# The seams of the feed-forward, and 16 rows with high and low part in one stationary operand

## The chip, the core and the metric

The kernel runs on one core of a Trainium2 chip. The metric is the time of one execution in microseconds (us) on the device. Five engines work side by side and wait for each other through semaphores: PE multiplies matrices, DVE, ACT and POOL work on elements, SP issues the transfers.

## The reference

1024 tokens of width 1024 get 16 learned rows in front (the meta rows), 1040 rows in all. Everything is float32.

```python
h = concatenate([meta, x])                       # 1040 x 1024
y = conformer_mixer(h, ...)                      # (c * silu(z)) @ w_out + b_out
h = layer_norm(ALPHA * h + y)
y = gla_mixer(h, ...)                            # u = h @ w_in, split in q, k, v, r, a1; a scan over chunks
h = layer_norm(ALPHA * h + y)[16:]
h = h + rms_norm(attention_and_pool(rms_norm(h)) @ w_out)
hn = rms_norm(h)
ff = (silu(hn @ w_gate) * (hn @ w_up)) @ w_down  # 2816 channels = 22 blocks of 128
h = h + rms_norm(ff)
e = rms_norm(p @ w_ple_proj)
out = h + sigmoid(h @ w_ple_gate) * e
```

## The kernel before, in words

**High and low parts.** A float32 product is made of three products of rounded parts: each operand is split in a high part (`xh`, a cast) and a low part (`xl`, the rest), and PE adds high x high, high x low and low x high. ACT or POOL makes a high part, DVE or POOL the low one. The stationary operand of a matmul has 128 rows and up to 128 columns, the moving one up to 512 columns.

**Token tiles.** `TILES` holds one tile of 16 rows (the meta rows) and eight of 128. A tile's rows are the columns of the stationary operand. For tile 0 PE takes 128 columns as for all others; only 16 rows of the product are used.

**The convolution's output** (`conv_out_*`). PE multiplies the gated rows by `w_out`, tile by tile, each into two PSUM banks (`CO_BANK`). Tiles 0 and 1 are cut into pieces (`early`, `rest`), and the steps of the variance over channels (`variance_parts`, `_sums`, `_spread`) stand between them; DVE and ACT turn these into mean, root and SiLU for the later chunks of columns (`CHUNKS4`). DVE then adds the residual and the bias and makes the layer norm of each tile (nine steps, L1013 to L997), in the order of tiles. PE turns the finished tile (`turn`, through one pair of banks), ACT and DVE make high and low part (`high`, `low`). Every order is written out by hand; a semaphore counts the steps of each kind.

**GLA's values** (`gla_in_*`). For each of four heads PE makes nine token tiles of 256 columns (`token_tile`), ACT copies them out. Keys are turned and multiplied by the values into a state (`gla_tensor`); for the meta rows over 16 rows.

**The feed-forward** (`ffn_*`). 22 blocks of 128 channels. Block 0 is made the usual way. Blocks are then taken in pairs of half-size products over sums of operands (seven products in place of eight; `OP_AT`, `ACT_OF`, `sum_h`, `sum_l`). `body(i)` makes the seven products of one round and, between them, the 16 down products (`down(p, n)`) of the block before; DVE adds these to `ff_acc` (`add_down`), and gives PSUM free (`dn_left`). `body` runs 20 times, 18 of them in a loop. `ff_low` makes the low half of a block's activations on DVE, after ACT's high half. At the entry DVE also makes four sums (`sum_begin`, `sum_rest`); at the exit the last block's 16 down products follow without anything between them, then p is embedded (`embed`), the first row tile normed and turned, and multiplied by `w_ple_gate`, split by ACT (`ple_high`) and POOL (`ple_l`, 16 operations at L2563). Then each of the eight row tiles goes through turn, product, sigmoid and output.

## Time and profile before

| | |
|---|---|
| time, median of 3 runs | 2177.44 us (2175.85 to 2179.28) |
| time of the profiled execution | 2184.11 us |
| its span, first to last instruction | 2182.4 us |
| mean granted clock of TensorE | 0.995 |
| PE busy | 2136.0 us, 98% |
| PE weight loads | 1847.7 us, 85% |
| DVE, ACT, POOL busy | 1264.2, 810.4 and 1031.2 us |

Times in rows are us from the start of the span. A line number is that of the kernel before. A row of the order of time gives start, duration, engine, line, operation, output and inputs, and in brackets how long the engine stood before it and who ended that. Matmuls overlap: the duration of one is longer than the distance to the next. The granted clock is a share of the full 2.4 GHz; 0.5 is the lower level, 1.2 GHz.

### The profile page before, as it was taken

The page shows a single profiled execution, that of the slowest core. Times are in us where ns is not written, and L with a number is a line of the kernel's source. Part 1 is how long each engine was busy: PE and PEld are TensorE (multiplying, and loading weights), DVE is VectorE, ACT ScalarE, POOL GpSimd, SP SyncE. Part 2 cuts the span into 40 slices and gives each one's busy share as a digit, 9 for nine tenths or more (in the row PEclk, how much of TensorE's full clock was granted, in tenths as well). Part 3 has the DMA queues.
Part 4 walks back from the last instruction along what each step waited for, and adds up shares of the span by engine and source line. Part 5 has one row for each costly group of instructions (what it writes and reads, how often), then busy time and mean ns, then how long its engine had stood idle before and what let it go on. Part 6 is the DMA issues. An engine that isn't in the chain of part 4 may idle for free.

```text
span 2182.4 us, 31664 instructions
## 1 busy us (share of the span) xinstructions
PE 2136.0 (98%) x12224; PEld 1847.7 (85%) x12224; DVE 1264.2 (58%) x1668; ACT 810.4 (37%) x1319; POOL 1031.2 (47%) x718
## 2 busy tenths in 40 slices
PE   6999999999999999999999999999999999999898
PEld 6999987899999998888787778878888888888687
DVE  1899998900039975640016545866656666566753
ACT  3444554112148852220226754432222222222453
POOL 1788950142237745022295630255555655555500
PEclk9999999999999999999999999999999999999999
DMA  4111122421100024221302022111111111112321
GB/s 139 41 57 39 41 94 73 124 72 39 40 20 1 1 78 145 80 75 39 117 1 84 2 97 106 49 39 57 49 58 58 38 57 49 58 58 64 138 78 48
DMA packets 128555, 136.65 MB, mean 63 GB/s; under 512 B 7008, under 2 KB 113248, under 8 KB 128318
## 3 DMA queue, kind: packets, MB, share of 16 engines
q1 hardware_dynamic: 128446, 135.11, 18.9%
q8 instruction: 79, 1.29, 0.2%
q14 instruction: 30, 0.25, 0.0%
HBM read 118.29 MB, written 16.81 MB: 62 GB/s over the span
## 4 chain that ended last, share of the span: by engine, by line
PE 88%; POOL 3%; DVE 3%; issue 2%; ACT 2%; DMA 1%; SPq 0%; POOLq 0%; ACTq 0%; DVEq 0%
PE PS L369 47%; PE PS L2590 18%; PE PS L1932 3%; POOL side_sum L582 2%; PE PS L1972 2%; PE PS L1943 2%; PE PS L1985 2%; PE PS L408 2%; PE PS L419 2%; PE PS L2313 1%; PE PS L1234 1%; PE PS L1267 1%; PE PS L1645 1%; POOL wl L345 1%; PE PS L391 1%
## 5 line engine op out<-in xcount | busy, mean ns | idle before, releaser
L2779 DVE TENSOR_TENSOR ff_acc<-ff_acc,PS 128x512 f32<-128x512 f32 x336 | 226.5, 686 | 191.9 <-PE PS L369 191.3
L369 PE MATMUL PS<-xh,wh 128*128 128x352 f32 (+2 forms) x944 | 287.7, 336 | 5.1 <-DVE xl L481 4.0
L369 PE MATMUL PS<-xl,wh 128*128 128x352 f32 (+2 forms) x944 | 285.9, 334 | 0.0
L369 PE MATMUL PS<-xh,wl 128*128 128x352 f32 (+2 forms) x944 | 285.4, 334 | 0.0
L2515 POOL TENSOR_TENSOR xl<-raw,xh 128x512 fp32r<-128x512 f32 x120 | 164.4, 1378 | 140.4 <-ACT xh L2644 140.4
L627 DVE SCALAR_TENSOR_TENSOR PS<-glu,conv_vec,PS 128x1040 f32<-128x1040 f32 (+2 forms) x196 | 228.5, 1236 | 1.1
L369 PE MATMUL PS<-wh,xh 128*128 128x256 f32 (+1 forms) x744 | 217.0, 314 | 1.3 <-ACT r_silu L1537 0.6
L369 PE MATMUL PS<-wl,xh 128*128 128x256 f32 (+1 forms) x744 | 215.8, 313 | 0.0
L369 PE MATMUL PS<-wh,xl 128*128 128x256 f32 (+1 forms) x744 | 215.3, 312 | 0.0
L369 PEld LDWEIGHTS PS<-xh,wh 128*128 128x128 f32 x944 | 174.9, 188 | 13.2 <-issue 5.8
L369 PEld LDWEIGHTS PS<-xl,wh 128*128 128x128 f32 x944 | 174.6, 188 | 8.0
L369 PEld LDWEIGHTS PS<-xh,wl 128*128 128x128 f32 x944 | 174.4, 188 | 7.7
L350 POOL CAST wh<-raw 128x2048 fp32r<-128x2048 f32 x15 | 28.5, 1897 | 300.4 <-PE PS L369 143.8
L2644 ACT CAST xh<-raw 128x512 fp32r<-128x512 f32 x120 | 72.5, 619 | 236.9 <-PE PS L2590 142.1
L345 POOL TENSOR_TENSOR wl<-raw,wh 128x2048 fp32r<-128x2048 f32 x30 | 138.8, 4628 | 34.7 <-ACT wh L341 33.5
L369 PEld LDWEIGHTS PS<-wh,xh 128*128 128x128 f32 x744 | 138.8, 188 | 10.7 <-ACT v_meta L1145 1.1
L369 PEld LDWEIGHTS PS<-wh,xl 128*128 128x128 f32 x744 | 140.1, 188 | 9.2
L369 PEld LDWEIGHTS PS<-wl,xh 128*128 128x128 f32 x744 | 139.8, 188 | 9.3
L2507 POOL TENSOR_TENSOR raw<-raw 128x512 f32<-128x512 f32 x80 | 115.2, 1441 | 48.7 <-DMA raw<-in_w_ffn_up_dram 42.7
L369 PE MATMUL PS<-dnh,ffh 128*128 128x512 f32 x336 | 131.7, 392 | 3.1 <-POOL dnl L2520 2.8
L369 PE MATMUL PS<-dnh,ffl 128*128 128x512 f32 x336 | 131.3, 391 | 0.0
L369 PE MATMUL PS<-dnl,ffh 128*128 128x512 f32 x336 | 131.3, 391 | 0.0
(426 smaller groups left out, 4952.2 us busy)
## 6 DMA issues: line engine op xcount, KB each, us to landing
rows<-h_rows SPq DMA_DIRECT2D x24, 512.0 KB, 3.4
dn_raw<-in_w_ffn_down_dram SPq DMA_DIRECT2D x22, 512.0 KB, 3.5
raw<-in_gla_w_in_dram SPq DMA_DIRECT2D x10, 1024.0 KB
raw<-in_w_ffn_gate_dram SPq DMA_DIRECT2D x20, 512.0 KB
raw<-in_w_ffn_up_dram SPq DMA_DIRECT2D x20, 512.0 KB
raw<-in_conv_w_in_dram SPq DMA_DIRECT2D x16, 512.0 KB
raw<-in_w_in_dram SPq DMA_DIRECT2D x8, 1024.0 KB
h_rows<-rows SPq DMA_DIRECT2D x16, 512.0 KB, 2.6
```

The costliest lines, as they stand in the source:

```text
L345: nc.gpsimd.tensor_tensor(wl[slot][:], raw_of(u)[0][:], wh[slot][:].bitcast(F32), ALU.subtract).then_inc(unit_ready, 1)
L369: last = nc.tensor.matmul(out_of(c, cn), s, x[:, c0:c0 + cn], start=n == 0 and m == 0, stop=n == len(terms) - 1 and m == 2)
L408: ins = nc.tensor.matmul(PS[:, bank + half, :], act_of(k), w_of(k)[:, half * HALF:(half + 1) * HALF], start=first and k == 0, stop=last an ...
L419: last = nc.tensor.transpose(blocks(bank)[:, k, 0:rows], src[0:rows, k * P:(k + 1) * P], ident[0:rows, 0:rows])
L582: ins = nc.gpsimd.tensor_tensor(acc[:], acc[:], tap_part[n % 3][:], ALU.add)
L627: ins = nc.vector.scalar_tensor_tensor(out=y, in0=x, scalar=w, in1=y, op0=ALU.mult, op1=ALU.add)
L1932: return nc.tensor.matmul(out, x, w[:, k, cols], start=begin, stop=end)
L2507: nc.gpsimd.tensor_tensor(out, a, b, op).then_inc(pool_own.sem, 1)
L2515: nc.gpsimd.tensor_tensor(lo, OP_AT[o], hi.bitcast(F32), ALU.subtract).then_inc(unit_ready, 1)
L2590: ins = nc.tensor.matmul(PS[:, OP_BANK[o], :], s[:, k, :], x[:, k, :], start=k == 0 and m == 0, stop=k == 3 and m == 2)
L2644: nc.scalar.copy(ring(o)[0], OP_AT[o]).then_inc(unit_hi, 1)
L2779: nc.vector.tensor_tensor(x, x, PS[:, dn_bank(p, n), :], ALU.add).then_inc(dn_left, 1)
```

## The change

It has three parts.

**The meta rows.** The 16 rows' high part, 16 columns of zeros and their low part stand side by side in one stationary operand of 48 columns (`conv_meta`, `h1_meta`). Multiplied by the high and by the low part of the weights it gives two row groups of the product, which are added later: for the convolution's output ACT copies the second group out (`meta_shift`), POOL adds the bias, DVE adds both; for the values they stay apart (`v_meta` has 48 rows), and the keys are stored twice, with zeros between, so that the product over 48 rows adds them. Tile 1's pieces now stand where tile 0's did, banks 0 and 6 change places, and the first turns go through bank 0.

**The entry of the feed-forward.** DVE makes the first low half of block 1's activations before the last step of the fourth sum.

**The exit.** The last block's down products are issued in pieces, with `embed(0)` after ten and `turn(0)` after fourteen of them. DVE and ACT take their steps in that order (`last_down`, `last_low`). `ple_high(act, 1)` comes after the first norm; `p_h`, the activations of the last stage and its banks lie elsewhere.

```diff
@@ -13,6 +13,7 @@
 D = 1024
 SEQ = 1024
 META = 16
+MROWS = 48
...
@@ -125,8 +126,11 @@
         raw_d = at("raw_d", [P, KT, T], A0)[:, :, CHUNKS4[3][0]:CHUNKS4[3][0] + UNIT]
         CO_SLOTS = (0, 5, 1, 2)
         MID_TURN = {4: 4, 6: 6, 7: 4}
-        CO_BANK = (0, 6, 4, 2, 0, 4, 2, 0, 4)
+        CO_BANK = (6, 0, 4, 2, 6, 4, 2, 6, 4)
+        turn_bank3 = lambda t: 0 if t < 6 else 6
         slot3 = [silu_z[:, :, c:c + P] for c in (0, 128, 272, 400, 528, 656)]
+        meta_shift = silu_z[0:META, :, 784:784 + P]
+        conv_meta = at("conv_meta", [P, KT, T + PAD], Z0, F32R)[:, :, 48:48 + MROWS]
...
@@ -142,12 +146,13 @@
...
-        v_meta = at("v_meta", [META, D], S0 + 2 * SLOT + 6144)
+        v_meta = at("v_meta", [MROWS, D], S0 + 2 * SLOT + 6144)
...
+        h1_meta = at("h1_meta", [P, KT, MROWS], W0 + 8192 + 2048, F32R)
...
@@ -209,11 +214,11 @@
...
-        p_h = at("p_h", [P, 2, SEQ], Z0 + 32768, F32R)
+        p_h = at("p_h", [P, 2, SEQ], O0 + 20480, F32R)
...
@@ -817,6 +822,10 @@
...
+            act.wait_ge(gated_lo, 1)
+            nc.scalar.copy(conv_meta[:, :, 0:META], xh[:, :, 0:META])
+            nc.scalar.copy(conv_meta[:, :, META:32], glu[:, :, 0:32 - META])
+            nc.scalar.copy(conv_meta[:, :, 32:MROWS], xl[:, :, 0:META]).then_inc(meta_packed, 1)
...
+            act.wait_ge(dense_done, 1)
+            act.wait_ge(conv_gated, len(CHUNKS4))
+            nc.scalar.copy(meta_shift, blocks(CO_BANK[0])[32:MROWS]).then_inc(meta_packed, 1)
...
+            pool.wait_ge(gain_in, 48)
+            pool.wait_ge(meta_packed, 2)
+            nc.gpsimd.tensor_tensor(meta_shift, meta_shift, gain3[0][0:META], ALU.add).then_inc(meta_packed, 1)
...
@@ -875,7 +890,7 @@
             def turn(t):
                 pe.wait_ge(h1_done, t + 1)
                 after(pe, part_lo, t, H1)
-                turn_blocks(rows3[t % 3], TILES[t][1], 6).then_inc(turned, 1)
+                turn_blocks(rows3[t % 3], TILES[t][1], turn_bank3(t)).then_inc(turned, 1)
...
+            def meta(ks):
+
+                for k in ks:
+                    for w in range(2):
+                        for half in range(2):
+                            ins = nc.tensor.matmul(PS[0:MROWS, bank_of(0) + half, :], conv_meta[:, k, :],
+                                                   of_slots(CO_SLOTS, k)[w][:, half * HALF:(half + 1) * HALF],
+                                                   start=k == 0 and w == 0, stop=k == KT - 1 and w == 1)
+                if ks[-1] == KT - 1:
+                    ins.then_inc(dense_done, 1)
...
-            early(0, xh, 0, first=True)
-            early(0, xh, 1)
+            early(1, xh, 0, first=True)
+            early(1, xh, 1)
             mean_last(pe, 1, 4, 2)
             mean_last(pe, 3, 3)
-            early(1, xh, 0, first=True)
-            early(1, xh, 1)
+            pe.wait_ge(gated_lo, 1)
+            early(1, xl, 0)
             variance_parts(pe, 1)
-            pe.wait_ge(gated_lo, 1)
-            early(0, xl, 0)
+            pe.wait_ge(meta_packed, 1)
+            meta(range(3))
             variance_sums(pe, 1)
-            early(1, xl, 0)
+            meta(range(3, 4))
             variance_parts(pe, 2)
             variance_spread(pe, 1)
             pe.wait_ge(unit_ready, U_CO + 4)
-            rest(0, range(4, 6))
+            meta(range(4, 6))
             variance_sums(pe, 2)
             variance_parts(pe, 3)
             variance_spread(pe, 2)
             variance_sums(pe, 3)
-            rest(0, range(6, KT))
+            meta(range(6, KT))
             rest(1, range(4, 6))
             variance_spread(pe, 3)
             rest(1, range(6, KT))
@@ -942,6 +968,7 @@
...
+                    pe.wait_ge(meta_packed, 2)
...
+                if t == 8:
+                    pe.wait_ge(dense_left, 8)
...
+                if t == 0:
+                    dve.wait_ge(meta_packed, 3)
+                dve_own.step(dve, nc.vector.tensor_tensor(x[0:n], x[0:n], gain3[0] if t else meta_shift, ALU.add))
                 layer_norm_rows(dve, x, n, t + 1, gain3[1], gain3[2]).then_inc(h1_done, 1)
...
-                    token_tile(h % 2, c0, 3 + q % 3).then_inc(gv_tile, 1)
+                    if t == 0:
+                        pe.wait_ge(meta_packed, 4)
+                    (token_tile(h % 2, c0, 3 + q % 3) if t else meta_tile(h % 2, 3 + q % 3)).then_inc(gv_tile, 1)
+
+        def meta_tile(slot, bank):
+
+            for k in range(KT):
+                for w in (wh, wl):
+                    last = nc.tensor.matmul(PS[0:MROWS, bank, 0:UNIT], h1_meta[:, k, :], w[slot][:, k, :],
+                                            start=k == 0 and w is wh, stop=k == KT - 1 and w is wl)
+            return last
 
...
+            dve.wait_ge(dense_done, 9)
+            nc.vector.tensor_copy(h1_meta[:, :, 0:META], xh[:, :, 0:META])
+            nc.vector.tensor_copy(h1_meta[:, :, 32:MROWS], xl[:, :, 0:META])
+            nc.vector.memset(h1_meta[:, :, META:32].bitcast(F32), 0.0).then_inc(meta_packed, 1)
...
-                    nc.scalar.copy(dst, PS[0:n, 3 + q % 3, 0:GV]).then_inc(gv_left, 1)
+                    nc.scalar.copy(dst, PS[0:n if t else MROWS, 3 + q % 3, 0:GV]).then_inc(gv_left, 1)
...
-                        last = nc.tensor.matmul(out_bank(6, h), k_rows[c % 2][0:n, h, :], v[:, h * GV:(h + 1) * GV], start=True, stop=True)
+                        last = nc.tensor.matmul(out_bank(6, h), k_rows[c % 2][0:n if c else MROWS, h, :], v[:, h * GV:(h + 1) * GV], start=True, stop=True)
...
-            nc.scalar.copy(k_rows[c % 2][0:n].rearrange("p h t -> p (h t)"), PS[0:n, 0, :]).then_inc(k_rows_done, 1)
+            for r in (32, 0) if c == 0 else (0,):
+                last = nc.scalar.copy(k_rows[c % 2][r:r + n].rearrange("p h t -> p (h t)"), PS[0:n, 0, :])
+            last.then_inc(k_rows_done, 1)
...
+            nc.gpsimd.memset(k_rows[0][0:MROWS], 0.0)
...
-            for n in range(HALVES):
-                down(LAST, n)
...
+                if last:
+                    act.wait_ge(p_turned, 1)
+                    nc.scalar.copy(p_h[:].rearrange("p k t -> p (k t)"), banks(0, 4)).then_inc(p_ready, 1)
...
-            ple_high(act, 1)
...
+                if n == 4:
+                    ff_low(1, 0, A_)
...
+            def last_low(i):
+                last_down(dve, 0, 2)
+                ff_low(i + 2, 1, C_)
+                last_down(dve, 2, 6)
...
-                ff_low(i + 2, 1, C_)
+                if last:
+                    last_low(i)
+                else:
+                    ff_low(i + 2, 1, C_)
...
-            ff_low(1, 0, A_)
...
-            body(FPAIRS - 3)
-            add_down(LAST, 0, 12)
+            body(FPAIRS - 3, True)
...
-            add_down(LAST, 12, HALVES)
+            last_down(dve, 6, 10)
...
-            pe.wait_ge(gain_in, G9 + 32)
+                turn_row(ff_acc[:, j, :], P, 2).then_inc(h4_turned, 1)
+
+            def act_cols(x, k):
+                return x[:, k // 4, (k % 4) * P:(k % 4 + 1) * P]
+
+            for n in range(10):
+                down_last(pe, n)
             pe.wait_ge(p_ready, 2)
             pe.wait_ge(w_low, DN0 + 2 * FPAIRS + 1)
+            embed(0)
+            for n in range(10, 14):
+                down_last(pe, n)
+            turn(0)
+            for n in range(14, HALVES):
+                down_last(pe, n)
+            pe.wait_ge(matrix_lo, M9 + 4)
+            pe.wait_ge(dn_left, 2 + LAST * HALVES + 14)
+            pe.wait_ge(act9_hi, 1)
+            dense_stage(lambda k: act_cols(act9h[0], k), lambda k: ple_h[k // 4][:, k % 4, :], out_bank9(0), first=True)
+            pe.wait_ge(act9_lo, 1)
+            dense_stage(lambda k: act_cols(act9l[0], k), lambda k: ple_h[k // 4][:, k % 4, :], out_bank9(0))
+            turn(1)
+            dense_stage(lambda k: act_cols(act9h[0], k), lambda k: ple_l[k // 4][:, k % 4, :], out_bank9(0), last=True).then_inc(dense_done, 1)
+            embed(1)
             pe.wait_ge(dn_left, 2 + FPAIRS * HALVES)
-            embed(0)
-            turn(0)
-            pe.wait_ge(matrix_lo, M9 + 4)
-
-            pe.wait_ge(act9_hi, 1)
-            dense_stage(lambda k: act9h[0][:, k, :], lambda k: ple_h[k // 4][:, k % 4, :], 0, first=True)
-            dense_stage(lambda k: act9h[0][:, k, :], lambda k: ple_l[k // 4][:, k % 4, :], 0)
-            turn(1)
-            pe.wait_ge(act9_lo, 1)
-            dense_stage(lambda k: act9l[0][:, k, :], lambda k: ple_h[k // 4][:, k % 4, :], 0, last=True).then_inc(dense_done, 1)
-            embed(1)
             for j in range(1, NX):
                 if j + 1 < NX:
                     turn(j + 1)
...
+            ple_high(act, 1)
...
+            last_down(dve, 10, HALVES)
+            low(0)
...
```

## Rows read from the trace of the kernel before

**Rows 1.** The page's first part: busy time and share of the span of each engine

```profile
...
PE 2136.0 (98%) x12224; PEld 1847.7 (85%) x12224; DVE 1264.2 (58%) x1668; ACT 810.4 (37%) x1319; POOL 1031.2 (47%) x718
...
```

**Rows 2.** Busy time (and count) of each engine from 1800 to 2000 us, with clock and DMA

```profile
...
1800.00:2000.00 200.00, 200.00 (x873) 162.26 (x872) 121.89 (x178) 51.24 (x91) 115.43 (x87) 1.00 0.18 53
...
```

**Rows 3.** The chain of work, 290 to 445 us: start, us, what

```profile
...
344.74 11.12 PE PS L369 x48
...
428.44 7.68 PE PS L369 x48
...
```

**Rows 4.** The chain of work, 440 to 660 us

```profile
...
521.45 7.57 PE PS L391 x48
...
538.87 68.42 PE PS L369 x576
...
```

**Rows 5.** PE in order of time, 1422 to 1445 us; in brackets the idle time and its end

```profile
...
1424.51 0.39 PE L2590 MATMUL PS<-xh,xl 128*128 128x512 f32 x1
1427.65 0.77 PE L369 MATMUL PS<-dnh,ffh 128*128 128x512 f32 x1 [2.75 <-POOL dnl L2520]
...
1434.04 0.40 PE L2590 MATMUL PS<-sum_h,xh 128*128 128x512 f32 x1
...
```

**Rows 6.** PE in order of time at the end of the feed-forward

```profile
...
2037.21 0.70 PE L369 MATMUL PS<-xl,ffh 128*128 128x512 f32 x2 [1.32 <-DVE ffl L2788]
...
2052.29 0.77 PE L369 MATMUL PS<-xl,p_h 128*128 128x512 f32 x1 [2.74 <-DVE ff_acc L2779]
...
2061.46 5.50 PE L408 MATMUL PS<-ple_h,act9h 128*128 128x512 f32 x16 [2.42 <-ACT act9h L2950]
...
```

**Rows 7.** The engines in a stretch of 2 us; the granted clock stands before the DMA share

```profile
...
1430.00:1432.00 2.00, 2.00 (x6) 1.57 (x5) 0.07 (x1) 0.00 (x0) 1.84 (x3) 0.50 0.00 0
...
```

**Rows 8.** ACT in order of time, 290 to 470 us

```profile
...
323.00 2.78 ACT L780 ACTIVATE conv_sq<-glu 128x3072 f32<-128x3072 f32 x1 [0.40 <-DVE glu L740]
...
335.66 0.17 ACT L789 ACTIVATE stat<-PS 128x3 f32<-128x3 f32 x1 [2.76 <-PE PS L718]
...
357.03 2.77 ACT L771 CAST xh<-glu 128x3072 fp32r<-128x3072 f32 x1 [4.74 <-DVE glu L755]
...
428.48 1.01 ACT L1029 CAST xh<-PS 128x1024 fp32r<-128x1024 f32 x1 [3.21 <-PE PS L426]
...
```

**Rows 9.** POOL in order of time, 290 to 360 us

```profile
...
291.72 2.02 POOL L589 TENSOR_TENSOR tile_sum<-tile_sum,glu 128x1040 f32<-128x1040 f32 x1
...
```

**Rows 10.** DVE in order of time, 355 to 470 us

```profile
...
360.19 1.20 DVE L1013 SCALAR_TENSOR_TENSOR silu_z<-silu_z,PS 16x1024 f32<-16x1024 f32 x1
...
429.53 1.23 DVE L1006 TENSOR_TENSOR xl<-PS,xh 128x1024 fp32r<-128x1024 f32 x1 [1.66 <-ACT xh L1029]
430.67 1.21 DVE L1013 SCALAR_TENSOR_TENSOR silu_z<-silu_z,PS 128x1024 f32<-128x1024 f32 x1
...
```

**Rows 11.** DVE in order of time, 1396 to 1452 us

```profile
...
1422.61 3.27 DVE L2760 TENSOR_TENSOR sum_l<-sum_f,sum_l 128x2048 fp32r<-128x2048 f32 x1
1425.80 2.35 DVE L2788 TENSOR_TENSOR ffl<-scratch,ffh 128x512 fp32r<-128x512 f32 x2
...
```

**Rows 12.** ACT in order of time, 1396 to 1452 us

```profile
...
1422.27 1.14 ACT L2660 CAST ffh<-scratch 128x512 fp32r<-128x512 f32 x2 [0.89 <-PE PS L369]
...
```

**Rows 13.** POOL in order of time, 1396 to 1452 us

```profile
...
1420.39 3.34 POOL L2520 TENSOR_TENSOR dnl<-dn_raw,dnh 128x512 fp32r<-128x512 f32 x1
1425.47 1.54 POOL L2520 TENSOR_TENSOR dnl<-dn_raw,dnh 128x512 fp32r<-128x512 f32 x1 [1.74 <-ACT dnh L2648]
...
```

**Rows 14.** ACT in order of time, 2014 to 2066 us

```profile
...
2039.20 3.71 ACT L2738 CAST ple_h<-ple_raw 128x2048 fp32r<-128x2048 f32 x2
...
```

**Rows 15.** DVE in order of time, 2014 to 2066 us

```profile
...
2047.48 2.28 DVE L2846 TENSOR_TENSOR xl<-PS,p_h 128x2048 fp32r<-128x2048 f32 x1
...
2053.84 2.18 DVE L2984 TENSOR_TENSOR ff_acc<-ff_acc,rows 128x1024 f32<-128x1024 f32 x1
...
```

**Rows 16.** POOL in order of time, 2014 to 2066 us

```profile
...
2033.88 23.27 POOL L2563 TENSOR_TENSOR ple_l<-ple_raw,ple_h 128x512 fp32r<-128x512 f32 x16
```

54 lines of the change are left out of this document (33 added, 21 removed).

## The prediction

> **What bounds the kernel now.** I read the page's first part, then the chain of work that ended last, then the timelines of the engines around the four places that the diff touches. PE is busy for 98% of the span [rows 1], and in the loop over the feed-forward pairs for all of it [rows 2]. So the kernel ends when PE has done its list: time can be won by matmuls that are taken out where nothing else is late, and where PE stands still. The chain through the convolution's output consists of PE alone [rows 3], and so does that through GLA's values [rows 4]. Two places have real holes: the start of the feed-forward, one wait of 2.75 us [rows 5], and its end, waits of 1.32, 2.74 and 2.42 us [rows 6]. After the long holes the granted clock is 0.5 for some us (the 1.2 GHz level of the two) [rows 7]: from 1427.65 to 1434.04 [rows 5] PE starts 15 matmuls of 512 columns, 0.426 us each, where the loop has 200 us / 872 = 0.23 us. A hole costs more than its length.
>
> **Part A, the meta tile of the convolution's output.** Before: 8 blocks x 3 products x 2 halves = 48 matmuls for 16 rows. After: the stationary operand has 48 columns (16 high, 16 zero, 16 low), so 8 x 2 x 2 = 32. The moving side keeps 512 columns, 11.12 us / 48 = 0.232 us each [rows 3]: 16 x 0.232 = 3.7 us less on PE. Three things can hold that back.
> (1) The variance steps are woven between these matmuls. Ahead of the third variance sum 12 matmuls go (60 before, 48 after), 2.8 us; but PE, 8 matmuls earlier there (about 325.3), now comes to the second big chunk's squares 0.5 us before ACT has them, 323.00 + 2.78 = 325.8 [rows 8]; so 2.3 us are left. From that sum the chain goes through the root at 335.66 [rows 8], SiLU, gate, high and low part to token tile 2. PE's own list is 3.7 - 0.5 = 3.2 us ahead there; it will wait a little for the low part: 3.1 us (2.3 if that chain is later than I think).
> (2) New steps stand in DVE's chain. The low product sits in PSUM partitions 32 to 47: ACT copies it (16x1024; the 128x1024 copy out of PSUM takes 1.01 us [rows 8]), POOL adds the bias (the nearest row is 128x1040 with 2.02 us [rows 9]), DVE waits for it. ACT's gated_high(3) would end at 357.03 + 2.77 - 2.3 = 357.5, so the sum is there at 357.5 + 1.0 + 2.0 + 0.1 = 360.6. DVE's first step began at 360.19 and took 1.20 [rows 10]; 2.3 us earlier it ends at 359.1. DVE waits 1.5 us, and its chain over the nine tiles is only 0.8 us ahead of before. It has no other hole until 427.87 (the 1.66 us in front of 429.53, [rows 10]). Bounds of the unseen POOL add: nothing, and twice 2.0 us: a chain 2.3 us ahead, or 1.2 us behind.
> (3) Does PE meet that chain? Before, part(1,0) started at 428.44 + 7.68/2 = 432.28 [rows 3], DVE freed its bank at 430.67 + 1.21 = 431.9 [rows 10]: a slack of 0.4 us, most of it because DVE itself waited 1.66 us. After: PE wants the bank at 432.28 - 3.1 = 429.2; DVE has low(6) at 427.87 - 0.8 + 1.2 = 428.2, and the bank free at 429.4. PE waits 0.2 to 0.3 us. Part A: 2.8 us; bounds 0.8 (the dear POOL add: the bank is free at 431.4, 2.2 us after PE wants it) and 3.7. The three small ACT copies that pack the operand lie in a wait of ACT for DVE, 5.2 us long before; uncovered they would cost their own 0.8 us at most (the 0.17 to 0.3 us of such small ACT rows, [rows 8]). The turns through other banks are the same transposes.
>
> **Part B, GLA's values for the meta rows.** Four heads, 24 matmuls of 256 columns become 16: 32 fewer. 68.42 us / 576 = 0.119 us each [rows 4], so 3.8 us. Whether 48 stationary columns make a matmul dearer: the 32-column narrow tile takes 7.57 / 48 = 0.158 us for 352 columns [rows 4], a little under the width's share; I take no difference. The three DVE operations that pack h1, POOL's memset and ACT's second copy of the keys lie beside a tile of 24 matmuls (2.9 us) or more. If one were uncovered I put it at 0.6 us, a half of an ACT cast twice as wide [rows 8]. Part B: 3.8, bounds 3.2 and 3.8.
>
> **Part C, the start of the feed-forward.** PE stops in front of down(1, 0), which needs the low half of the activations. DVE makes it (two 128x512 in 2.35 us from 1425.80) only after the last subtraction of sum 4 (3.27 us from 1422.61) [rows 11]. The change puts the first half in front of that subtraction. ACT has the high half at 1422.27 + 0.6 [rows 12]. The half will be there at about 1424.4, PE needs it at 1424.51 + 0.23 = 1424.74 [rows 5]: the hole goes, 1427.65 - 1424.74 = 2.9 us. With it goes the low clock, which lasted to 1434.04 [rows 5, 7]: 15 matmuls in 6.4 us instead of 3.4, 3.0 us. What is late next: the subtraction, 2.3 to 3.3 us, runs to 1426.7 or 1427.7, the second half (0.7 to 1.2) to 1427.4 or 1428.9, the first add_down (0.7) to 1429.2 if I lean to the later; down(1, 2) wants it after 18 more matmuls, at 1428.8: a wait of 0.4 us, too short for the clock (the 1.32 us hole at 2037.21 did not lower it, [rows 6]). Part C: 5.9 - 0.4 = 5.5 us. Bounds: 4.0 if PE waits again at the third and fourth operand, which POOL makes; 5.9.
> POOL and DVE slow each other here: the subtraction takes 3.27 us instead of 2.3, with POOL's dnl at the same time [rows 11, 13]. The Trainium skill, page SBUF — State Buffer, section "SBUF: two separate sides", has the two share a port pair as an exclusive lock, held for the whole instruction by whoever starts first, when DVE has two SBUF inputs. The trace agrees: POOL's dnl, queued at 1420.39, takes 3.34 us and the next 1.54 [rows 13]. By that rule the wait of 0.4 us comes; if the two didn't hinder each other, ffl(1, 1) would be there by 1427.4, down(1, 2) would not wait, and part C would be 5.9 us, the sum 16.8.
>
> **Part D, the end of the feed-forward.** The 16 down products of the last pair, embed(0) and turn(0) are now woven: ten downs, embed(0), four, turn(0), two, then the dense product. The norm of row tile 0 starts as soon as its two halves are in. I replayed it with the durations of before. PE starts at 2037.21 as before [rows 6]. ACT copies p_h before the second ffh, inside a wait for DVE; ple_high(1), 3.71 us from 2039.20 before [rows 14], now comes after the first norm, at about 2042.8. DVE: two adds, ffl, four adds, p_l (2.28, [rows 15]) to about 2045.8; PE has then waited 1.2 us for embed(0). Four adds, the norm of tile 0 (up to 2.18 us for its last step beside POOL [rows 15]) to 2052.2; PE waits 0.9 us for turn(0), then has the last two downs at 2054.5. In front of the dense product the program waits for all of ple_l. POOL makes that in 16 operations, 23.27 us from 2033.88, so to 2057.15 [rows 16]. POOL's list isn't touched and it was not waiting; the later ple_high(1) is done at 2046.5, before POOL comes to it. So PE starts the dense product at 2057.2 instead of 2061.46 [rows 6]: 4.3 us. It stands 2.7 us before that, so I take the low clock once more, as behind the 2.42 us hole of before, where 16 matmuls took 5.50 us [rows 6] instead of 16 x 0.23 = 3.7 (1.8 us, of which I count 1.7). Part D: 4.3 us. If the clock stays up, 4.3 + 1.7 = 6.0; if it stays down for 6 us as at 1428, 3.0; if DVE or POOL is 1 us later as well, 2.0. From there on all is as before, with PE full.
>
> **Sum.** 2.8 + 3.8 + 5.5 + 4.3 = 16.4 us. The profiled execution took 2184.11 us (span 2182.4 and 1.7 around it), so 2167.7; it stands 6.7 us above the median of the runs, 2177.44. I take the saving off the median: 2161.0 us. Ends: least 0.8 + 3.2 + 4.0 + 2.0 = 10.0, 2167.4; most 3.7 + 3.8 + 5.9 + 6.0 = 19.4, 2158.0.
>
> **The rivals.**
> - The clock stays high at the end (the three shorter holes don't lower it): for it, the hole of 1.32 us did not; against it, the last is 2.7 us. 18.1 us, 2159.3. Chance 0.25.
> - DVE's chain sets the convolution's output, because POOL's add or the wait in front of it is dearer, and POOL's operands come late in the first pair: A 0.8, C 4.0, D 4.3: 12.9 us, 2164.5. For it, the slacks of 0.4 us; against it, that POOL has to be late in two places at once. Chance 0.15.
> - The merged operand doesn't save what it says (a matmul with 48 stationary columns, or one that waits for its load, costs half as much again): A and B give nothing; 9.8 us, 2167.6. Against it the narrow tile [rows 4]. Chance 0.05.
> - Slower: the pair loop runs in another phase of POOL against DVE and PE gets a wait in each of its 18 turns. To undo 16.4 us and lose 4.4 us more takes 20.8 / 18 = 1.16 us a turn; from there it decides, at 1.3 us a turn the time is 2184. For it, the loop's lateness at entry changes and POOL's operations stretch beside DVE. Against it, PE has no hole in 200 us [rows 2] with POOL busy 58%, and a loop bound by PE falls back into its own phase. Chance 0.03.
> - The forecast, 2159.5 to 2163: 0.50.
>
> **The numbers.** 0.2% is 4.4 us, about what a measurement of this kernel can tell. The forecast and the first three rivals are all faster by more than that: 0.50 + 0.25 + 0.15 + 0.05 = 0.95; no difference 0.02, for what I haven't seen, slower 0.03. The range takes both ends of the sum, 2158.0 and 2167.4, and up to 1 us for the scatter of the runs (1.8 us around their median): 2157 to 2168.
>
> **What would show it.** In the profile of after: 48 matmuls fewer; token tile 2 starts about 3 us earlier, at 341.7, DVE waits about 1.5 us before its first bias add, part(1, 0) has at most a short wait; the values stage is 208 matmuls and 24.7 us a head instead of 216 and 25.7; no wait above 0.7 us between 1400 and 1430 (of the old time) and clock 1.0 there; at the end holes of about 1.2, 0.9 and 2.7 us, the last one ended by POOL's ple_l. It would be wrong with a new hole in the first pair or in the loop, or if the clock's low stretches move to other places.

## The result, and the profile after

| | runs | median, us | lowest to highest |
|---|---|---|---|
| before, on the same chip | 9 | 2180.44 | 2175.85 to 2189.18 |
| after | 9 | 2169.49 | 2167.41 to 2172.80 |

The ratio is 0.9944, 95% interval 0.9929 to 0.996: 0.56% faster, 11 us by the medians. The forecast was 16.4 us and 2161.0 us. The range ended at 2168, so the time lies 1.5 us outside it. The profiled execution of after took 2170.98 us (span 2169.3), that of before 2184.11 (2182.4): 13.1 us between them.

The first part of the page after, which answers to [rows 1]:

```profile
...
PE 2125.5 (98%) x12176; PEld 1835.9 (85%) x12176; DVE 1265.1 (58%) x1671; ACT 812.1 (37%) x1324; POOL 1034.3 (48%) x720
...
```

48 matmuls are gone, as they should be. PE was busy 10.5 us less and stood still 2.6 us less.

**Before the first edit.** The same step stands at 306.98 us before and 308.83 us after, though nothing ahead of it was changed. The 1.85 us are made at the start, where the clock fell in this execution and not in that of before. The lines give the stretch, then the busy time of PE, its loads, DVE, ACT and POOL; the granted clock is the last number but two:

```profile
...
34.00:38.00 4.00, 2.63 (x19) 2.37 (x17) 0.29 (x1) 1.33 (x2) 0.00 (x0) 1.00 0.00 0
38.00:42.00 4.00, 2.92 (x10) 2.95 (x11) 0.93 (x1) 1.93 (x2) 2.45 (x1) 0.60 0.00 0
...
```

**Part A.** The chain of work of after, 306 to 450 us, answers to [rows 3]:

```profile
...
343.59 11.38 PE PS L374 x48
...
399.10 1.03 PE PS L431 x8
...
414.92 1.06 PE PS L431 x8
...
427.98 7.96 PE PS L374 x48
...
441.52 8.63 PE PS L374 x55
```

Token tile 2 starts 1.15 us earlier by the trace, 3.0 with the 1.85 of the start. Then 0.9 us is given back in four short waits: 11.38 instead of 11.12, turns of 1.03 and 1.06 instead of 0.87, 7.96 instead of 7.68. From ACT's first gate step (308.73) to its first copy of a GLA projection (449.19) it is 140.46 us; before it was 142.50 (306.88 to 449.38). Part A gave 2.05 us. DVE and POOL in order of time show why:

```profile
...
359.77 1.20 DVE L1042 SCALAR_TENSOR_TENSOR silu_z<-silu_z,PS 16x1024 f32<-16x1024 f32 x1
363.06 1.21 DVE L1047 TENSOR_TENSOR silu_z<-silu_z 16x1024 f32<-16x1024 f32 x1 [2.09 <-POOL silu_z L855]
...
387.96 5.42 DVE L1047 TENSOR_TENSOR silu_z<-silu_z 128x1024 f32<-128x1024 f32 x1
...
```

```profile
...
360.56 2.40 POOL L855 TENSOR_TENSOR silu_z<-silu_z 16x1024 f32<-16x1024 f32 x1 [7.19 <-ACT silu_z L844]
...
387.71 4.59 POOL L350 TENSOR_TENSOR wl<-raw_z,wh 128x2048 fp32r<-128x2048 f32 x1
...
```

DVE waits 2.09 us for POOL's addition of 2.40 us on 16 rows (I had 1.5 and 2.0). With the 1.85 us of the start counted, its chain is only 0.2 us ahead of before from there on (363.06 against 361.43), where I had 0.8. 25 us later an addition that otherwise takes 1.23 us takes 5.42 beside POOL's subtraction. That one is in the kernel before too (5.43 us); it costs nothing there, and can cost something now that PE is ahead.

**Part B.** The meta tiles of GLA's values answer to [rows 4]:

```profile
...
537.69 17.32 PE PS L374 x144
555.01 1.87 PE PS L1161 x16
...
579.61 1.84 PE PS L1161 x16
...
```

16 matmuls in 1.85 us where 24 took 24 x 0.119 = 2.85. From ACT's first GLA copy to DVE's weight cast behind the values it is 182.07 us (449.19 to 631.26) instead of 186.01 (449.38 to 635.39): 3.9 us.

**Part C.** DVE at the feed-forward's start, against [rows 11]:

```profile
...
1419.01 1.28 DVE L2861 TENSOR_TENSOR ffl<-scratch,ffh 128x512 fp32r<-128x512 f32 x1 [0.42 <-ACT ffh L2716]
1420.21 2.28 DVE L2828 TENSOR_TENSOR sum_l<-sum_f,sum_l 128x2048 fp32r<-128x2048 f32 x1
1422.42 1.77 DVE L2861 TENSOR_TENSOR ffl<-scratch,ffh 128x512 fp32r<-128x512 f32 x1
...
```

The first half is there first, PE has no hole, and the clock is 1.00 where it was 0.50 [rows 7]. PE's work that began at 1435.57 us before begins at 1425.87: 9.7 us earlier, and 4.0 of these were there already (1410.21 against 1406.20). So 5.7 us between these two traces.

**The loop.** From there to the turn of `p` (2033.98 and 2024.17) the lead stays 9.8 us. PE is busy 199.99 of the 200 us of [rows 2].

**Part D.** PE in order of time at the feed-forward's end, against [rows 6]:

```profile
...
2027.05 0.70 PE L374 MATMUL PS<-xl,ffh 128*128 128x512 f32 x2 [0.97 <-DVE ffl L2861]
...
2032.19 0.70 PE L374 MATMUL PS<-xl,ffh 128*128 128x512 f32 x2 [0.78 <-DVE ff_acc L2804]
...
2036.09 0.50 PE L374 MATMUL PS<-xl,p_h 128*128 128x512 f32 x1 [0.94 <-DVE xl L2920]
2042.21 1.09 PE L424 MATMUL PS<-ident,ff_acc 128*128 128x128 f32 x8 [0.39 <-DVE ff_acc L3069]
2048.28 9.19 PE L413 MATMUL PS<-ple_h,xl 128*128 128x512 f32 x32 [3.58 <-POOL ple_l L2611]
...
```

The waits have moved, not gone: 6.7 us in sum, 7.4 before (6.5 in [rows 6] and one of 0.90 at 2041.09). The last is longer than the 2.7 us I had, and the clock falls behind it:

```profile
...
2048.00:2050.00 2.00, 1.72 (x6) 1.40 (x7) 1.93 (x4) 0.25 (x1) 0.22 (x1) 0.81 0.00 0
2050.00:2052.00 2.00, 2.00 (x6) 1.52 (x6) 1.71 (x3) 1.10 (x3) 0.00 (x0) 0.50 0.00 0
...
```

The dense product starts 13.2 us earlier than before, 3.4 more than the 9.8 brought along. In sum: 2.05 + 3.9 + 5.7 + 3.4 - 1.85 = 13.2, the 13.1 us between the spans. So much for the two traces. What the runs' medians hold of it, the experiments had to tell.

### The profile page after: what moved, and what is told of

Same layout as the page of the kernel before. It is cut to its first block, busy times and chain, and to the rows that moved or that the text cites. A ratio compares the mean times of both kernels' runs of the same rounds, so it can differ in the third digit from the quotient of the medians.

```text
span 2169.3 us, 31582 instructions
## 1 busy us (share of the span) xinstructions
PE 2125.5 (98%) x12176; PEld 1835.9 (85%) x12176; DVE 1265.1 (58%) x1671; ACT 812.1 (37%) x1324; POOL 1034.3 (48%) x720
## 4 chain that ended last, share of the span: by engine, by line
PE 62%; POOL 17%; issue 15%; DVE 3%; ACT 2%; DMA 1%; POOLq 0%; SPq 0%; DVEq 0%; ACTq 0%
PE PS L374 38%; POOL xl L2563 6%; POOL raw L2555 5%; PE PS L1980 3%; POOL side_sum L587 2%; PE PS L2020 2%; PE PS L1991 2%; PE PS L2033 2%; PE PS L1312 2%; PE PS L413 2%; PE PS L424 2%; PE PS L1279 2%; PE PS L2361 2%; POOL dnl L2568 1%; PE PS L1693 1%
## 5 line engine op out<-in xcount | busy, mean ns | idle before, releaser
L2847 DVE TENSOR_TENSOR ff_acc<-ff_acc,PS 128x512 f32<-128x512 f32 x320 | 216.4, 686 | 185.4 <-PE PS L374 184.9
L374 PE MATMUL PS<-wh,xh 128*128 128x256 f32 (+1 forms) x712 | 208.1, 316 | 1.4 <-ACT v_meta L1190 0.5
L374 PE MATMUL PS<-wl,xh 128*128 128x256 f32 (+1 forms) x712 | 206.8, 314 | 0.0
L374 PE MATMUL PS<-wh,xl 128*128 128x256 f32 (+1 forms) x712 | 206.3, 313 | 0.0
L374 PEld LDWEIGHTS PS<-wh,xh 128*128 128x128 f32 x712 | 132.7, 188 | 11.1 <-ACT v_meta L1190 1.1
L374 PEld LDWEIGHTS PS<-wh,xl 128*128 128x128 f32 x712 | 134.1, 188 | 9.2
L374 PEld LDWEIGHTS PS<-wl,xh 128*128 128x128 f32 x712 | 133.8, 188 | 9.3
```

The costliest lines, as they stand in the source:

```text
L374: last = nc.tensor.matmul(out_of(c, cn), s, x[:, c0:c0 + cn], start=n == 0 and m == 0, stop=n == len(terms) - 1 and m == 2)
L2847: nc.vector.tensor_tensor(x, x, PS[:, dn_bank(p, n), :], ALU.add).then_inc(dn_left, 1)
```

## The experiments

Eighteen experiments with sixteen kernels; all_again and state_16_again are all_fixes and state_16 once more. In a name, "no" takes one part out of the changed kernel and "only" puts one into the kernel before; the five that begin with "all" have both mends, which are told below. Times in us; "ratio" is to the kernel before on the same chip, with its 95% interval; the last column counts runs with a mean granted clock of 0.994 or less. Beside the experiments the kernel before has 100 runs on five chips: median 2182.05, 2175.7 to 2192.3, 31 of them at 0.994 or less.

The groups were measured on different chips. The median of before lies between 2181.3 and 2183.3 on them, and a kernel measured twice gave 2163.17 and 2164.13, another one 2177.95 and 2174.16. A difference of medians of 1 or 2 us, as they are given below, tells little by itself; the stretches of the traces are the firmer figures.

| kernel | median | lowest to highest | ratio | low clock |
|---|---|---|---|---|
| no_conv_meta | 2172.38 | 2169.2 to 2173.9 | 0.9952 (0.9936 to 0.9968) | 0 of 6 |
| no_gla_meta | 2179.26 | 2171.8 to 2184.9 | 0.9985 (0.9969 to 1.0002) | 6 of 12 |
| no_ff_start | 2173.26 | 2171.5 to 2177.1 | 0.9964 (0.9947 to 0.998) | 0 of 7 |
| no_tail | 2170.28 | 2169.4 to 2172.6 | 0.9945 (0.993 to 0.996) | 0 of 6 |
| state_16 | 2177.95 | 2170.6 to 2180.9 | 0.9969 (0.9952 to 0.9986) | 8 of 12 |
| state_48 | 2175.38 | 2174.4 to 2179.4 | 0.9972 (0.9959 to 0.9986) | 0 of 12 |
| tail_late | 2164.67 | 2163.3 to 2166.1 | 0.9918 (0.9899 to 0.9938) | 0 of 6 |
| conv_dve | 2169.22 | 2167.0 to 2173.9 | 0.9943 (0.9923 to 0.9964) | 0 of 6 |
| before_48 | 2182.14 | 2177.5 to 2188.4 | 0.9987 (0.9972 to 1.0003) | 1 of 12 |
| only_gla_meta | 2173.62 | 2171.7 to 2183.2 | 0.9958 (0.9939 to 0.9976) | 1 of 10 |
| only_tail | 2179.79 | 2175.9 to 2185.5 | 0.9986 (0.9971 to 1.0002) | 2 of 12 |
| all_fixes | 2163.17 | 2161.7 to 2163.8 | 0.9902 (0.9881 to 0.9924) | 0 of 6 |
| all_again | 2164.13 | 2163.1 to 2165.9 | 0.9912 (0.9889 to 0.9935) | 0 of 6 |
| all_state_16 | 2163.47 | 2162.8 to 2164.6 | 0.991 (0.9887 to 0.9933) | 0 of 6 |
| all_ff_start | 2167.69 | 2164.5 to 2168.7 | 0.9926 (0.9902 to 0.9949) | 0 of 6 |
| all_gla_24 | 2167.52 | 2166.1 to 2173.4 | 0.9931 (0.9906 to 0.9956) | 0 of 6 |
| state_16_again | 2174.16 | 2168.8 to 2179.7 | 0.9964 (0.9948 to 0.998) | 6 of 12 |
| conv_16 | 2170.53 | 2168.6 to 2180.5 | 0.9951 (0.9936 to 0.9966) | 3 of 10 |

### One part undone at a time

The edit is the part's own piece of the diff, turned back. For the feed-forward's start:

```diff
-                if n == 4:
-                    ff_low(1, 0, A_)
...
+            ff_low(1, 0, A_)
             ff_low(1, 1, C_)
```

> The changed kernel with the convolution output's part undone (the meta tile again takes 48 matmuls of 512 columns); the other three parts stay. Reading of the two traces: the part is worth 2.05 us, because 2.8 us of matmuls went and about 1 us came back as short waits for VectorE inside the later tiles; so this kernel should take about 2171.5 us, and the tiles should run without those waits (the first 48 matmuls 11.12 us instead of 11.38, the transposes at 399 and 415 us 0.87 instead of 1.03 and 1.06, the block at 428 us 7.68 instead of 7.96). The prediction's term: 2.8 us, so 2172.3 us. Rival (the term is no property of the part, the offset of 1.85 us that stands before it is): the time from the gate to the first GLA projection is the same as in the changed kernel, 2169.5 us.

Measured 2.9 us above the changed kernel. The trace has 142.53 us from the gate to the first GLA copy, and 140.43 to 140.55 in the three kernels that keep the part: 2.0 to 2.1 us in every pair.

> The changed kernel with GLA's part undone (four meta tiles of the values take 24 matmuls each again). Reading of the traces: 3.9 us, so about 2173.4 us, with the four tiles taking 2.84 us each instead of 1.85. The prediction's term: 3.8 us. Rival: TensorE is not the bound there (the values' tiles wait for weights or for their copies), then the time stays at 2169.5 us and idle time stands beside the tiles.

Measured 9.8 us above, more than twice what either theory gave. The values' stretch is 186.0 us in its trace, so 3.9 of it are the matmuls. The rest is in the twelve runs' spread, and in the trace it is low clock. The first lines are of PE in order of time, the others are stretches of 2 us:

```profile
...
633.97 1.16 PE L1275 MATMUL PS<-qk 128*128 128x128 f32 x8 [0.46 <-ACT v_rows L1175]
635.50 1.99 PE L1319 MATMUL PS<-v_meta,k_rows 16*128 16x256 f32 x8
...
```

```profile
...
636.00:638.00 2.00, 2.00 (x12) 1.51 (x12) 1.97 (x4) 0.59 (x1) 0.00 (x0) 1.00 0.00 0
638.00:640.00 2.00, 2.00 (x13) 1.64 (x11) 2.00 (x5) 0.67 (x1) 0.00 (x0) 0.68 0.00 0
640.00:642.00 2.00, 2.00 (x11) 2.00 (x10) 1.12 (x3) 1.97 (x4) 1.11 (x2) 0.50 0.00 0
...
```

PE has no hole from the products on: it is busy all the time, and the clock falls behind these eight products of 16 rows. The wait of 0.46 us just before them is there in the changed kernel too, where the clock stays at 1.00. These are GLA's first state product, `k_rows` times `v_meta`. Part B made it 48 rows, an edit that I had priced at nothing. The 9.8 us are so not the part's worth in the kernel before alone; the next section takes them apart.

> The changed kernel with only the order at the feed-forward's start undone: the low part of the first half of pair 1's activations is again made behind the last combination's low part. Reading of the traces: 5.7 us, so about 2175.2 us, with the hole of 2.75 us at the second down product and TensorE's granted clock at 0.50 for some 6 us behind it. The prediction's term: 5.5 us. Rival: the hole comes back, and the clock stays at 1.00 (2.9 us, so 2172.4 us), or the loop of the pairs takes up the delay at its first turns (0 to 1 us).

Measured 3.8 us above, between theory and rival, and the runs fall in two groups: four at 2171.5 to 2173.3, three at 2176.2 to 2177.1. The trace is of the first kind, with the same hole and the clock up:

```profile
...
1420.79 0.47 PE L374 MATMUL PS<-dnh,ffh 128*128 128x512 f32 x1 [2.75 <-POOL dnl L2568]
...
```

```profile
...
1419.00:1421.00 2.00, 0.21 (x1) 0.24 (x2) 2.00 (x3) 0.22 (x1) 1.14 (x1) 1.00 0.00 0
1421.00:1423.00 2.00, 2.00 (x10) 1.64 (x10) 0.98 (x2) 0.88 (x2) 1.04 (x1) 1.00 0.77 262
...
```

So the hole comes here too, without the low clock behind it; in the profiled execution of before it came with it. What brings the three slower runs, at a mean clock of 0.995, no trace shows.

> The changed kernel with the feed-forward's end undone (all 16 last down products in one block, then embedding, turn, and the dense product's three stages, high operand first). Reading of the traces: 3.4 us, so about 2172.9 us, with the dense product starting behind GpSimd's last low part as before. The prediction's term: 4.3 us, so 2173.8 us. Rival (the 1.85 us that the changed kernel lost before its first edit belongs to the edits): then the stretch before 300 us is 1.85 us shorter in one of these four kernels and not in the others.

Measured 0.8 us above (the means differ by 1.0), not 3.4. The stretch before 300 us is short in all four kernels (the gate at 305.4 to 307.1 us), so the 1.85 us don't belong to an edit: the rival falls.

### The rows of the state product, and the two mends

The first edit of two:

```diff
-                    v = v_meta if c == 0 else v_rows[:, c - 1, :]
+                    v = v_meta[0:META] if c == 0 else v_rows[:, c - 1, :]
                     for h in range(GH):
-                        last = nc.tensor.matmul(out_bank(6, h), k_rows[c % 2][0:n if c else MROWS, h, :], v[:, h * GV:(h + 1) * GV], start=True, stop=True)
+                        last = nc.tensor.matmul(out_bank(6, h), k_rows[c % 2][0:n, h, :], v[:, h * GV:(h + 1) * GV], start=True, stop=True)
```

That is state_16, on the changed kernel. state_48 is no_gla_meta with the matmul's `0:n if c else MROWS` of the changed kernel, a `v_meta` of 48 rows and two memsets ahead of it:

```diff
+            nc.vector.memset(v_meta[:], 0.0).then_inc(meta_packed, 1)
...
+            nc.gpsimd.memset(k_rows[0][0:MROWS], 0.0)
```

> The changed kernel with GLA's first state product on the 16 rows of the high part alone, as before the change (the kernel so leaves the low part of the meta tile's values out of the state); the merged projections stay. The runs so far: without GLA's part the twelve runs lie between 2171.8 and 2184.9 us with mean granted clocks of 0.999 to 0.991, with it all runs of four kernels lie at 0.995 or above. In the one profile of the kernel without it the clock fell to 0.50 at 639 us, just behind the eight state products of 16 rows. Theory 1 (these 16-row products bring the clock down in some executions, the merged tile's 48 rows do not): the runs spread over some 10 us, median about 2174 to 2176 us, clocks down to 0.991 to 0.994 in a third of them or more. Theory 2 (the low clock comes from the projections of the meta tile with 16 stationary columns, or from where the stage falls in time): 2169.5 us, spread 5 us, clocks 0.996 and above, as in the changed kernel.

> The changed kernel with GLA's part undone (24 matmuls for each meta tile of the values, 3.9 us more) but the first state product on 48 rows, the added rows zero. Theory 1 (the 16-row products bring the clock down): the spread of the kernel without GLA's part goes, median about 2169.5 + 3.9 = 2173.4 us, clocks of 0.996 and above, and the difference to the kernel without GLA's part (2179.3 us) is what the rows do. Theory 2 (the 16 stationary columns of the projections, or the place in time): the spread stays, 2172 to 2185 us, median about 2179 us.

Both as theory 1 said in spread and clock, but for one run of state_48 at 0.995; both medians lie 2 us above what was expected. The product takes 1.99 us with 16 rows and with 48. state_16 has eight of twelve runs at the low clock, and its trace has the fall at the same place, some 3 us behind the product's start, and the clock back at 1.00 some 20 us later:

```profile
...
631.39 1.99 PE L1334 MATMUL PS<-v_meta,k_rows 16*128 16x256 f32 x8
...
```

```profile
...
632.00:634.00 2.00, 2.00 (x13) 1.54 (x11) 1.97 (x4) 0.59 (x1) 0.00 (x0) 1.00 0.00 0
634.00:636.00 2.00, 2.00 (x11) 1.75 (x9) 2.00 (x5) 0.79 (x1) 0.00 (x0) 0.58 0.00 0
...
652.00:654.00 2.00, 2.00 (x11) 2.00 (x11) 1.25 (x3) 0.23 (x1) 2.00 (x4) 0.50 0.00 0
654.00:656.00 2.00, 2.00 (x16) 2.00 (x15) 1.97 (x3) 0.00 (x0) 2.00 (x4) 0.80 0.00 0
...
```

The same place in state_48, the product on 48 rows and the stretches behind it:

```profile
...
634.01 1.99 PE L1323 MATMUL PS<-v_meta,k_rows 48*128 48x256 f32 x8
...
```

```profile
...
636.00:638.00 2.00, 2.00 (x16) 1.74 (x15) 2.00 (x7) 0.45 (x2) 0.00 (x0) 1.00 0.00 0
638.00:640.00 2.00, 2.00 (x18) 2.00 (x19) 1.54 (x2) 2.00 (x3) 0.60 (x1) 1.00 0.00 0
...
```

state_48 lost the spread, and its median is 3.9 us below that of no_gla_meta; its trace has the clock at 0.70 from 825 to 830 us, another place.

The tail's mend:

```diff
-            pe.wait_ge(matrix_lo, M9 + 4)
+            pe.wait_ge(matrix_hi, M9 + 4)
             pe.wait_ge(dn_left, 2 + LAST * HALVES + 14)
...
             turn(1)
+            pe.wait_ge(matrix_lo, M9 + 4)
```

> The changed kernel with the dense product's wait for GpSimd's low part of the gate weights moved from before its first stage to before its third, the only one that reads it. The profile of the changed kernel: the last down product ends at 2044.7 us, the high part of the weights is there at 2036.1 and the activations' parts at 2044.4 and 2046.9, but the dense product starts at 2048.28, when GpSimd is done. Theory (GpSimd's chain sets this place, and the forecast's step on it was right): the hole of 3.6 us goes, and with it most of the low clock behind it (1.9 us): 4 to 5.5 us, so 2164 to 2165.5 us. Rival (VectorE's chain of the last additions and the second row norm, whose turn stands between the stages, sets it anyway): the wait moves to the turn, gain 1 us or less, 2168.5 us or more.

Measured 4.8 us less, and from the turn of `p` to the end its trace takes 140.3 us instead of 145.1. In the chain of work the dense product's first two stages follow without a hole, and at full clock:

```profile
...
2042.61 1.09 PE PS L424 x8
2043.70 1.40 PE PS L374 x6
2045.10 7.47 PE PS L413 x32
...
```

The convolution's mend, DVE's part; the last line is the split that POOL did before, and ACT now makes the cast for it:

```diff
                 if t == 0:
-                    dve.wait_ge(meta_packed, 3)
+                    dve.wait_ge(meta_packed, 2)
+                    dve_own.step(dve, nc.vector.tensor_tensor(x[0:n], x[0:n], meta_shift, ALU.add))
...
+                if t == 3:
+                    unit_low_vector(dve, U_GQK, QK_SLOTS[0])
```

> The changed kernel with two loads taken off VectorE's chain in the convolution's output: VectorE adds the meta tile's low part and bias itself (one operation of 1.2 us more) instead of waiting 2.09 us for GpSimd's addition of 2.40 us, and the weight unit that GpSimd splits at 386 us is split by ScalarE and VectorE (2.3 us), since VectorE's addition of two operands in SBUF took 5.42 us instead of 1.23 beside it. Theory (the part of the convolution gave 2.05 us instead of 2.8 because VectorE's chain became the later one for moments): the short waits of TensorE (0.26, 0.16, 0.19 and 0.28 us) go, the stretch from the gate to the first GLA projection's copy is 139.6 to 139.8 us instead of 140.46, so 0.7 to 0.9 us less. Rival (the waits are for PSUM banks and turns, not for VectorE's lateness): the stretch stays at 140.4 us.

As the theory said in the trace: the stretch is 139.73 us, the turns are 0.87 us each, the last block 7.68; of the four waits only the first is left (11.35). In the median it is 0.3 us, too little to tell from nothing. The edit takes both loads off DVE at once, so which of the two made the waits isn't shown; the first wait belongs to neither. DVE's addition that had taken 5.42 us took 1.23, and the split moved to DVE 2.28:

```profile
...
383.96 1.23 DVE L1049 TENSOR_TENSOR silu_z<-silu_z 128x1024 f32<-128x1024 f32 x1
...
389.51 2.28 DVE L354 TENSOR_TENSOR wl<-raw_z,wh 128x2048 fp32r<-128x2048 f32 x1
...
```

### The parts on the kernel before, and all mends together

The edits are those of state_48, and the parts' own pieces of the diff.

> The kernel before with nothing changed but the rows of GLA's first state product: 48 instead of 16, the added ones zero. No instruction goes on TensorE, and two memsets come. The kernel before has run 42 times so far: mean 2182.1 us, 2175.7 to 2192.2, mean granted clock at 0.994 or below in 13 of them. Theory (the 16-row products bring the clock down in some executions, at a cost of some 9 us each time): no run above about 2185 us or below a clock of 0.995, mean 2178.5 to 2179.5 us, about 3 us less. Rival (the spread comes from the place in time of GLA's first turn, which part B moved): the spread and the mean stay as in the kernel before.

A miss. One run of twelve is at 0.994 or less (0.993, 2188.4 us), against 31 of 100 without the edit and 8 of 27 on the same chip, but the median doesn't fall, and the mean by 0.3 us (2182.3 against 2182.6), not by 3. So on the kernel before no gain from the 48 rows is shown. Its trace has the clock at 0.50 from 1275 to 1280 us, in the attention, and down again at the feed-forward's start (0.66 from 1430 to 1435) and end (0.70 from 2050 to 2055).

> The kernel before with GLA's part alone. Theory (3.9 us of matmuls and the low clock behind the 16-row products): 3.9 us less than the kernel before with 48 rows, so a mean of about 2174.6 to 2175.6 us, with no clock below 0.995. Rival (its worth depends on the other parts, since taking it out of the changed kernel cost 9.8 us): 2172 to 2173 us.

8.4 us below the kernel before by the median, between theory and rival (2173.6); the mean, 2175.2, is what the theory said, though one run has a clock of 0.994. It lies 8.5 us below before_48 as well, where the matmuls account for 3.9. Both have the product on 48 rows, so the rest is something else. In the two traces it is mostly low clock at other places: the clock stayed at 1.00 here in the stretches of before_48's falls at the feed-forward's start and end. Whether that holds over the runs is open. Its trace has the order of the old tail at full clock, which I had not seen yet:

```profile
...
2045.28 0.47 PE L371 MATMUL PS<-xl,p_h 128*128 128x512 f32 x1 [2.74 <-DVE ff_acc L2798]
2049.07 1.09 PE L421 MATMUL PS<-ident,ff_acc 128*128 128x128 f32 x8 [0.79 <-DVE ff_acc L3003]
2051.98 3.91 PE L410 MATMUL PS<-ple_h,act9h 128*128 128x512 f32 x16 [1.82 <-ACT act9h L2969]
```

The dense product starts 24.69 us behind the turn of `p` (2027.29). In the profile before that was 27.48, in the one after 24.11.

> The kernel before with the feed-forward's end alone. The prediction's term: 4.3 us. Reading of ten profiles since: from the turn of the embedding's input to the end the old order took 148.4 and 147.3 us, the new one 145.0 to 146.8 (mean 145.9 of seven), so 1.4 to 2.5 us, and taking the part out of the changed kernel cost 1.0 us. So a mean about 1 to 2.5 us below that of the kernel before (2182.1 us), with its spread. Rival: the prediction's 4.3 us, 2177.8 us.

2.3 us below the kernel before; but it also had fewer of the low runs (2 of 12 for 31 of 100), which may be chance, and how much of the 2.3 us is the part's own isn't shown.

> The changed kernel with both mends: the dense product waits for the low part of its weights only before its third stage (2164.67 us alone), and VectorE's chain in the convolution's output is relieved (0.73 us less in that stretch of the trace, 2169.22 us alone). If they add: about 2164 us, the stretch from the gate 139.7 us, the tail 140.3 us. Rival (the relieved chain ends elsewhere): 2164.7 us as with the tail's mend alone.

2163.17 us: faster than both kernels, 0.98% below before. In the trace the two mends add: the stretch from the gate takes 139.75 us and the tail 139.8. By the median they give 1.5 us more than the tail's mend alone, about as much as two chips can differ.

### On the quiet kernel

The kernel with both mends stays within 3 us in each of its two sets of six runs, so terms can be read better there. all_gla_24 puts a first pass in front of each merged tile:

```diff
             for k in range(KT):
+                nc.tensor.matmul(PS[0:MROWS, bank, 0:UNIT], h1_meta[:, k, :], wh[slot][:, k, :], start=k == 0, stop=k == KT - 1)
+            for k in range(KT):
```

> The kernel with both mends once more, unchanged, as the base for the three others on the same chip. Six runs gave 2161.7 to 2163.8 us, all with a mean granted clock of 0.999: every theory expects 2163 us again, within 1 us, and so little spread that the others can be read to about 1 us.

> Both mends, and the feed-forward's start in the old order. Theory (the hole is there each time, the low clock behind it in some executions only): the lowest runs 2.8 us above the base, at 2165.8 us, others 2 to 3 us higher still, at 2168 to 2169 us. The prediction's term was the hole and the low clock together each time: all runs 5.5 us above the base, 2168.5 us. Rival: the hole alone, all runs at 2165.8 us.

> Both mends, and each merged tile of GLA's values preceded by eight more matmuls of the same shape (their result is overwritten), so 24 instead of 16; the state product stays on 48 rows. Theory (these matmuls are worth their own time, 32 x 0.119 us): 3.8 us above the base, 2166.8 us, with no more spread than the base. Rival (the low clock comes from the narrow projections): a wider spread, some runs 7 us or more above the base.

The base came again at 2164.13. all_ff_start is 3.6 us above it, its lowest run only 0.3, which no theory had, its highest 4.6: the trace has the hole (2.72 us) with the clock at 1.00. all_gla_24 is 3.4 us above, and the values' stretch 3.56 us longer: the matmuls' own time. But its spread is wider than the base's, with one run of six at 2173.4 us, 9 us above the base; what that run met isn't shown.

> Both mends, and GLA's first state product on the 16 rows of the high part alone (the low part of the meta tile's values is left out of the state). Theory (the product of 16 rows brings the clock down in some executions): the fastest runs at 2163 us like the base, half or more of them 7 to 10 us higher, with clocks of 0.993 to 0.996. Rival (the widening in the kernels so far came with other stretches, as the kernel before with 48 rows suggests, whose mean did not fall): the runs stay within 2161.5 to 2165 us.

None of six runs is low: the rival's case, and against theory 1 as I had it. So the last two:

> The changed kernel with the first state product on 16 rows, once more and unchanged. It had eight of twelve runs at a clock of 0.994 or below, while the same edit on the kernel with both mends had none of six, all at 0.998 and above. If the edit's effect hangs on the kernel around it (the place in time at which GLA's first turn comes), this one is wide again: some runs at 2176 to 2181 us. If the first result was the chip's state in that hour, it is now as narrow as the changed kernel: 2167 to 2173 us.

> The same 16-row product in the kernel with VectorE's relieved chain alone, which brings GLA's first turn 0.73 us earlier and leaves the tail as changed. If a shift of that size decides, its runs are narrow, 2167 to 2174 us, beside a wide kernel without the shift. If the tail's mend, which comes 1.4 ms later, is what went with the narrow runs, or if it is chance from run to run, this kernel has runs at 2176 us and above as well.

state_16_again is wide again: six low runs of twelve, in the mean 8.3 us above the others, with the fall at 634 us in its trace. conv_16 has three low runs of ten, and the fall at 636 us in its trace. So a shift of 0.73 us doesn't take it away.

All experiments with before and after: with 16 rows 56 of 164 runs have a clock of 0.994 or less, with 48 rows 2 of 98. A mean clock doesn't say where the clock was low; the traces do. All four traces whose mean clock is that low have the fall right behind the 16-row product; the three others with 16 rows (before, only_tail, all_state_16) don't have it, and none of the thirteen 48-row traces has one there. For the changed kernel it is shown that the rows matter: it had no low run in nine, state_16 had 14 in 24, and no_gla_meta went from 6 of 12 to 0 of 12 with 48 rows. That none of the six runs of all_state_16 had it is unlikely if its chance were one half as in state_16, but not if it were the 3 in 10 of conv_16; what sets the chance in one kernel and not in the other stays open, and so does why before_48 gained nothing. The place in time alone doesn't: the product starts at 630.09 and 631.39 us in two of the traces with the fall and at 630.90 in that of all_state_16, which has none.

## Why the prediction missed

The sign was right, and so were the matmuls taken out in A and B and the hole closed in C. The forecast failed in its base, in the start of the dense product (D), in the low clock that it took as part of every run (C), and by a smaller size in A.

- **Part A**, 2.8 forecast, 2.05 found: a size. Of the 3.1 us at token tile 2, 3.0 came, and the wait for POOL came too (2.09 for 1.5). The step that failed is the third, that PE would be held once, for 0.2 to 0.3 us. It was held there (0.28), and three times more, 0.9 us in all. I had looked for DVE's slack at one block, and its chain was 0.2 us ahead instead of 0.8; I had also not seen the 5.4 us addition on the way. conv_dve takes three of the four waits away.
- **Part B**, 3.8 forecast, 3.9 and 3.4 to 3.6 found. "POOL's memset" and the keys' second copy cost nothing, as said, but what they serve, the 48-row product, does more than an instruction count shows: in the changed kernel it keeps the clock up. In the kernel before a run with the low clock is 7.6 us above the others in the mean (2187.9 and 2180.3), and 31 in 100 are such, 2.4 us of the mean. How much of that the 48 rows give back isn't shown: before_48 gained 0.3 us in the mean. No row of the single trace could tell, for its clock was 1.00 in that stretch.
- **Part C**, 5.5 forecast: the hole, 2.7 to 2.8 us, each time, and up to 3 us more only where the clock falls; 3.6 and 3.8 by the medians. The step that failed is "with it goes the low clock": of six traces with the old order all have the hole (2.72 to 2.76 us), and two the low clock behind it. The wait at `down(1, 2)`, 0.4 forecast, was 0.2. POOL's `dnl` at 1421.48 was the one to be stretched (2.17 us), for DVE had begun first. That is in keeping with the Trainium skill, page SBUF — State Buffer, section "SBUF: two separate sides", by which whoever starts first holds the shared ports.
- **Part D**, 4.3 forecast, 0.8 by the median of no_tail. The step that failed is "PE starts the dense product at 2057.2 instead of 2061.46". The 2061.46 was itself late because of low clock in the old order: 27.48 us behind the turn of `p`, 24.69 where the clock stayed up. The new order should have started 23.2 us behind the turn; it starts at 24.11, because POOL was done 0.9 us later than I had replayed, and then takes 9.19 us for the 32 matmuls, where the old one took 7.54 at full clock. So at full clock the part gains 0.6 us and pays 1.6 for the low clock behind its own new hole of 3.58 us. From the turn to the end the old order took 144.0 to 148.4 us in four traces, the new one 144.6 to 146.8 in ten; the means, 146.1 and 145.8, hardly differ. tail_late shows what held it: POOL's low part, waited for two stages too early.
- **The base.** "I take the saving off the median" joined two things that don't belong together. The savings were measured on an execution 6.7 us slower than that median, and part of these 6.7 us was the low clock that C and D were paid for removing. The median itself, of three runs, was 3.0 us below that of nine, and 4.6 below that of a hundred.

The miss of 8.5 us so is about 3.0 of the base, 0.75 in A, 1.8 in C and 3.5 in D, together 9.0; the 0.5 us left over is smaller than the runs can tell. This sum takes A and B from the traces and C and D from the medians. By the medians alone the four parts taken out one at a time come to 17.3 us (2.9, 9.8, 3.8 and 0.8), more than the 11 us between the kernels, because without B the low clock comes in; so the division is an estimate, and the steps that failed are firmer than their shares.

Of the rivals, DVE's chain as the later one came true in part A in a mild form. Its other half, POOL's operands late in the first pair, did not, nor the merged operand that saves nothing, nor a loss in the loop. That the clock stays high at the end did not come true either: it fell there in all ten traces with the new order and the early wait.
